# Conditioning totals over partitions: TensorE transposes and VectorE sums in place of products with a column of ones

## The reference, cut to what matters

```python
def adaln_mod(cond, w, b):
    m = jax.nn.silu(cond) @ w + b
    m = m.reshape(m.shape[0], 1, 6, D_MODEL)
    return tuple(m[:, :, j] for j in range(6))

sh1_p, sc1_p, g1_p, sh2_p, sc2_p, g2_p = adaln_mod(c_ctx[None, :], ada_w[i], ada_b[i])
sh1_s, sc1_s, g1_s, sh2_s, sc2_s, g2_s = adaln_mod(c, ada_w[i], ada_b[i])
```

## Time and profile before

| | |
|---|---|
| median of 3 runs | 2580.86 us (2577.29 to 2583.99) |
| the profiled execution, its own time | 2578.82 us |
| its span in the trace | 2577.0 us |
| PE busy | 2324.0 us, 90% of the span |
| DVE busy | 1793.2 us, 70% |
| ACT busy | 1304.5 us, 51% |
| mean granted TensorE clock | 0.954 of full speed |

### The profile page before, as it was taken

The page is one execution under the profiler, slowest core; times in us unless marked ns, Lnnn a source line. Parts: engine busy times, 40 slices in busy tenths (PEclk is TensorE's granted clock), DMA queues, the critical chain, the costliest instruction groups (busy, mean ns, idle before and its releaser), DMA issues.

```text
span 2577.0 us, 28840 instructions
## 1 busy us (share of the span) xinstructions
PE 2324.0 (90%) x9896; PEld 1537.3 (60%) x9896; DVE 1793.2 (70%) x2348; ACT 1304.5 (51%) x1698; POOL 336.5 (13%) x229
## 2 busy tenths in 40 slices
PE   6999999999957999999998688998859999999995
PEld 2867868678634666666665355554436666666663
DVE  3665655656657999999998512332368999999996
ACT  3222212222235877778776323332238778777773
POOL 1000000000021122112111200000221113231102
PEclk9999999999977999999999789999979999999997
DMA  7443435434236988998887210000138998888892
GB/s 250 131 123 108 148 96 164 131 115 141 90 129 221 354 319 312 348 344 330 322 314 264 87 68 0 34 1 1 63 119 316 349 350 332 333 327 315 331 343 88
DMA packets 167646, 529.04 MB, mean 205 GB/s; under 512 B 13525, under 2 KB 22282, under 8 KB 167306
## 3 DMA queue, kind: packets, MB, share of 16 engines
q1 hardware_dynamic: 162954, 515.35, 55.5%
q0 software_dynamic: 2304, 8.39, 0.9%
q10 hardware_dynamic: 2304, 4.20, 0.4%
HBM read 516.72 MB, written 11.17 MB: 205 GB/s over the span
## 4 chain that ended last, share of the span: by engine, by line
PE 70%; DVE 12%; issue 6%; DMA 5%; ACT 5%; POOL 1%; SPq 0%; ACTq 0%; DVEq 0%
PE ps L1511 67%; DVE W_LO L1321 6%; PE ps L1514 3%; DMA RAW_W<-in_moe_w_down_dram 3%; DMA RAW_W<-in_moe_w_gate_dram 2%; ACT YE_HI L290 1%; ACT GATE L853 1%; ACT W_HI L290 1%; DVE YE_LO L1339 1%; DVE B L1366 1%; POOL SMALL L560 1%; DVE IDX L1296 1%; DVE MIXREG L1295 0%; POOL SMALL L559 0%; DVE B L1099 0%
## 5 line engine op out<-in xcount | busy, mean ns | idle before, releaser
L1321 DVE TENSOR_TENSOR W_LO<-RAW_W,W_HI 128x1024 fp32r<-128x1024 f32 x768 | 901.4, 1220 | 81.6 <-ACT W_HI L290 75.1
L290 ACT ACTIVATE W_HI<-RAW_W 128x1024 fp32r<-128x1024 f32 x768 | 779.0, 1055 | 286.4 <-PE ps L1511 166.4
L1511 PE MATMUL ps<-W_HI,XET_HI 128*80 128x512 f32 x1024 | 331.9, 406 | 37.9 <-DVE W_LO L1321 18.6
L1511 PE MATMUL ps<-W_LO,XET_HI 128*80 128x512 f32 x1024 | 326.7, 401 | 0.0
L1511 PE MATMUL ps<-W_HI,XET_LO 128*80 128x512 f32 x1024 | 325.5, 400 | 0.0
L1511 PEld LDWEIGHTS ps<-W_HI,XET_HI 128*80 128x80 f32 x1024 | 153.2, 152 | 125.6 <-DVE W_LO L1321 26.8
L1511 PEld LDWEIGHTS ps<-W_LO,XET_HI 128*80 128x80 f32 x1024 | 155.9, 152 | 89.4 <-issue 7.7
L1511 PEld LDWEIGHTS ps<-W_HI,XET_LO 128*80 128x80 f32 x1024 | 154.8, 151 | 87.7 <-issue 6.0
L1070 DVE SCALAR_TENSOR_TENSOR ADA_SUM<-ADA_RAW,NCOL,ADA_SUM 128x512 f32<-128x512 f32 x280 | 191.3, 747 | 0.1
L1511 PE MATMUL ps<-W_HI,HTE_HI 128*80 128x512 f32 x512 | 164.7, 403 | 11.2 <-issue 11.2
L1511 PE MATMUL ps<-W_LO,HTE_HI 128*80 128x512 f32 x512 | 160.1, 394 | 0.0
(11 more groups left out here) (218 smaller groups left out, 3584.2 us busy)
## 6 DMA issues: line engine op xcount, KB each, us to landing
RAW_W<-in_moe_w_gate_dram SPq DMA_DIRECT2D x128, 1024.0 KB, 5.3
RAW_W<-in_moe_w_up_dram SPq DMA_DIRECT2D x128, 1024.0 KB, 6.1
RAW_W<-in_moe_w_down_dram SPq DMA_DIRECT2D x128, 1024.0 KB, 7.2
ADA_RAW<-in_ada_w_dram SPq DMA_DIRECT2D x80, 512.0 KB, 3.7
RING_RAW<-in_ret_w_in_dram SPq DMA_DIRECT2D x48, 512.0 KB, 4.2
W<-in_ada_w_dram SPq DMA_DIRECT2D x4, 2048.0 KB, 14.2
RING_RAW<-in_ret_w_out_dram SPq DMA_DIRECT2D x16, 512.0 KB, 4.6
xn_rows<-B SPq DMA_DIRECT2D x8, 512.0 KB, 12.8
```

The lines of the kernel that those rows point to most:

```text
L290: return nc.scalar.activation(out, in_, ACT.Copy, scale=scale)
L1321: V_.tensor_tensor(W_LO[:, slot], RAW_W[:, (place + i) // 2 % RAWS, at:at + PART], W_HI[:, slot].bitcast(F32), ALU.subtract).then_inc(MS_[ ...
L1511: return T.matmul(out, lhsT, rhs, start=first, stop=last)
```

## The change

The sum over partitions is done in another way. PE transposes each 128 by 128 block of `ADA_SUM`, so that the 512 columns of one conditioning vector fill one whole bank: partition = output column within the block, free axis = four blocks of 128 former partitions. DVE then sums along the free axis with two `tensor_reduce` instructions (one for each c, 512 values in and 4 out per partition), waits for them, and adds the bias in a third instruction that reads SBUF.

As each event now fills two banks instead of eight columns of one, `COLS_BANK` holds pairs, and some waits of PE change: the second event of a head waits until DVE has read the first (both use banks 4 and 5); the third waits for one more evacuated tile of scores; the y loop waits for the sums of the third event ahead of its first product, since that writes bank 6; the fourth event waits for the gate's evacuation (bank 2) instead of for the third's sums; the value tiles 2 and 3 both wait for the fifth event of the head before; gate tile 2 waits for the second event's sums instead of the first's.

```diff
-        COLS_BANK = (4, 5, 3, 3, 6)
+        COLS_BANK = ((4, 5), (4, 5), (3, 6), (3, 2), (6, 7))
...
-                parts = ps[:, COLS_BANK[t], 0:8].rearrange("p (q c) -> p q c", q=4)
-                V_.tensor_tensor(cols, parts, BCOL[:, layer, at].unsqueeze(2).to_broadcast([P, 4, 2]), ALU.add).then_inc(ada2_col, 1)
+                for c in range(2):
+                    last = V_.tensor_reduce(cols[:, :, c], ps[:, COLS_BANK[t][c], :].rearrange("p (q n) -> p q n", q=4), AX, ALU.add)
+                chain.link(last)
+                V_.tensor_tensor(cols, cols, BCOL[:, layer, at].unsqueeze(2).to_broadcast([P, 4, 2]), ALU.add).then_inc(ada2_col, 1)
...
-                for q in range(4):
-                    for c in range(2):
-                        at = 2 * q + c
-                        last = mm(ps[:, COLS_BANK[t], at:at + 1], ADA_SUMS[C % 2][:, c, q * P:(q + 1) * P], ONES[:, 0:1], True, True)
+                for c in range(2):
+                    for q in range(4):
+                        at = slice(q * P, (q + 1) * P)
+                        last = tr(ps[:, COLS_BANK[t][c], at], ADA_SUMS[C % 2][:, c, at])
                 last.then_inc(ada2_tr, 1)
...
                     if k in (2, 6):
-                        pe.wait_ge(qk_ev, 4 * h + 4)
+                        pe.wait_ge(*((qk_ev, 4 * h + 4) if k == 2 else (ada2_col, NT * h + 1)))
                         ada_columns2(h, k // 4)
...
-                        if k == 0 and t == 2 and h:
+                        if k == 0 and t in (2, 3) and h:
                             pe.wait_ge(ada2_col, NT * h)
...
                     if k == 6:
-                        pe.wait_ge(sc_ev, NT * h + 3)
+                        pe.wait_ge(sc_ev, NT * h + 4)
                         ada_columns2(h, 2)
...
-                            pe.wait_ge(*((v_ev, NT * h + 5), (sc_ev, NT * h + 1), (ada2_col, NT * h + 1), (ada2_col, NT * h + 2), (sc_ev, NT * h + 2))[t])
+                            pe.wait_ge(*((v_ev, NT * h + 5), (sc_ev, NT * h + 1), (ada2_col, NT * h + 2), (ada2_col, NT * h + 2), (sc_ev, NT * h + 2))[t])
...
                 pe.wait_ge(kp_ev, h + 1)
+                pe.wait_ge(ada2_col, NT * h + 3)
...
                     if t == 0:
-                        pe.wait_ge(ada2_col, NT * h + 3)
+                        pe.wait_ge(silg, NT * (h + 1))
                         ada_columns2(h, 3)
```

## The result

The changed kernel takes 2561.25 us (median of 6 runs, 2555.44 to 2566.6) beside 2579.07 us for the kernel before on the same chip (2575.88 to 2586.96): ratio 0.9925, 95% interval 0.9905 to 0.9945. Measured twice more, in 5 rounds each, it gave 2567.3 against 2581.44 us (0.9939, 0.9921 to 0.9956) and 2565.17 against 2579.84 us (0.9943, 0.9928 to 0.9958). The forecast was 2564.5 us.

What follows compares the result with a forecast made beforehand. PE was taken to bound the kernel, carrying 70% of the chain. Savings of 15.6 and 0.97 less 1.34 us gave -15.2: 2563.6 from the profiled 2578.82, or 2565.6 by the median; forecast 2564.5, range 2558 to 2572.

Steps and rivals of the forecast that it cites:

- PE sets the pace in the heads: In the heads, PE is busy 100.00 of 100 us, so the end moves with PE's work, microsecond for microsecond.
- Sixteen matmuls (eight products in two passes) for eight transposes, 0.82 us saved: On PE, each event falls from 1.70 to 0.88 us; 19 events in the heads give 15.6 us.
- The sums on DVE, +1.34 us per event: Two reductions, a wait and the bias addition take 1.51 us on DVE where 0.165 stood; 27 us in all.
- What hides them: DVE's idle stretches behind events in the heads cover the added work at no cost; tightest, 1.40 us left before second y's statistics.
- The moved waits: PE's changed waits in the heads are already reached when PE comes to them, so they cost nothing visible.
- Behind the heads, +0.37 us: The last event saves 0.97 us on PE, but its uncovered DVE sums between `ROWI` and `OHP` add 1.34.
- the half-clock stretch of 1.7 us: Just behind the last event the clock halves for 3.4 us, costing 1.7 us; it may move by as much either way.
- The sum: Whole kernel: -15.6 - 0.97 + 1.34 = -15.2 us, giving 2563.6 from the profiled execution; forecast put at 2564.5.
- Two-pass transposes: Transposes on PE run as 16 records at 0.107 us, so the heads gain nothing: 2580 us; chance 7%.
- the failing cover: DVE's sums delay PE at the scores and second y in four heads; 10.7 us come back: 2574 us; chance 5%.
- the falling clock in the heads: Transposed events halve the clock for 3.4 us, 1.7 us lost each; 19 falls give 2596 us; chance 6%.
- the second rival: DVE's cover fails at scores and second y, 2574 us; at twice the reduction rate only (2.78 - 2.74) us exposed; 5%.

Runs made afterwards that it cites:

- the event of 32: Changed kernel with each transpose done four times, 32 transposes per event: 2618.49 us, heads 684.32 us.

## Why the prediction was right, point by point

**PE sets the pace in the heads.** Right. Repeating the transposes adds their full price to the stretch, at 0.108 us each, while repeating the sums once adds nothing.

**Sixteen matmuls (eight products in two passes) for eight transposes, 0.82 us saved.** The mechanism was right, the term too small: 0.91 us by both views. I had 1.70 right for what goes; what comes takes 0.80 instead of 0.88. The pitch of 0.108 us was right, as the repeated transposes show, but the product behind follows the last transpose sooner than a whole pitch: the event of 32 takes 3.41 us, that is 32 x 0.109 less some 0.08. By that the heads should gain 19 x 0.91 = 17.3 us; they gained 17.3 to 17.9, where 15.6 were forecast. The bound that transposes don't overlap (2.18 us per event) did not come true, and with it falls the estimate from the Trainium skill's page "TensorE: Matmul & The Clock Gate", section "Part 4: PE-mode transpose": its 275 ns, given for bf16, agree with the recorded duration of one (272 ns here, fp32), but are not what one costs in a row.

**The sums on DVE, +1.34 us per event.** Right: a reduction lasts 686 ns on average against 692 worked out, the pair to the addition 1.33 us. The Trainium skill's page "VectorE: DVE Perf Modes", section "Rules for kernel authors", calls the reduction the slowest operation of DVE and says to consider restructuring; here 40 of them cost 1.3 us of time in all, since 38 are hidden.

**What hides them.** Right in the heads. The row on which most rested was the tightest one, 1.40 us forecast ahead of the second y's statistics and 1.32 measured; doubling the sums uses it up without a cost. That what exceeds the idle time goes to PE was too strict: with the sums five times DVE is some 3.6 us late there and PE waits 2.55. My reading of the margins did not carry as far as five times, where two places came late instead of one.

**The moved waits.** Right: no PE wait stands on them in the changed kernel, and with the products put back in the new banks and waits the heads take what they took before.

**Behind the heads, +0.37 us.** The event's -0.97 came out at -0.85 (1.85 to 1.00) and the sums' +1.34 at +1.33 (0.66 to 1.99 us of waiting). What I had left open either way, the half-clock stretch of 1.7 us, went: -1.7. That it went was not foretold. Together -1.2 us, of which the stretch as a whole shows -0.7 to -1.4.

**The sum.** By the measured terms it is -17.3 - 1.2 = -18.5 us instead of -15.2, or 2560.3 against the profiled execution of before. The forecast of 2564.5 had 0.9 added for the median of before; the three medians, 2561.25, 2567.3 and 2565.17, lie on both sides of it. The gains by the medians are 17.8, 14.1 and 14.7 us: all below the 18.5 of the measured terms, two of them by some 4 us. So that the forecast's 15.2 came out so close is in part luck. Its terms were too small by 1.7 us in the heads and by 1.6 behind them, and the whole time shows, on average over the three, some 3 us less than the two stretches gained. That the shift is carried to the end is thus shown as far as the first expert product; whether a part is given back behind it or the difference is scatter stays open.

**The rivals.** Two-pass transposes are out by the count of records and by the repeated transposes, the failing cover by the doubled sums, the falling clock in the heads by the 32 transposes in a row. The 2.78 us that the second rival sets against 2.74 can't be rebuilt exactly from its own terms (2 x 1.34 is 2.68, four reductions of 692 ns are 2.77); by either, next to nothing would be exposed, and with the doubled sums PE gets no new wait in the heads. The cover does have an end, though, and what then comes back is more than the sum of the waits, as the five-fold sums show.

## What to carry to other kernels

Where one engine is busy without a gap, count what each instruction holds it for from start to next start among its neighbours, not by its recorded duration: a transpose of 272 ns costs 108 here, and an fp32 product that writes a single column costs that twice, once for each of its two passes. The idle time ahead of the other engine's instructions gives a first measure of how much work may move to it: here 1.2 us more per event cost nothing, and at 4.9 us more the waits came back at two places per head and took the clock with them. And look for the one place where the same step has no cover: it may be worth moving it alone.

## What the runs showed of the hardware that I had not expected

Behind 1.64 us of idle time and sixteen one-column matmuls the granted clock falls to 1.2 GHz, in all three profiles that have them behind the heads (with the products put back everywhere it falls shortly before the event ends). Behind the same idle time and eight transposes in the same place it stays at 2.4 GHz, in all six profiles that have them. The length of the event does not decide it: sixteen transposes take 1.87 us, as long as the sixteen matmuls with their 1.85, and the clock stays up. But transposes don't always keep it up: 32 of them behind 1.94 us of idle time ran at 0.50 from 774.90 to 778.00, while 32 in the full stream of the heads ran at 1.00. What separates these two cases was not tested. The Trainium skill's page "TensorE: Matmul & The Clock Gate", section "Part 4: PE-mode transpose", says that transposes don't count as busy for the clock as products do. The 32 behind the heads would fit that; the heads don't show it, and in the last event it was the products behind which the clock fell.

A wait of 2.5 us in an otherwise full PE halved the clock afterwards in three of four heads with the same instructions and the same wait, and not in the fourth. So a short wait can cost some 1.7 us more than its length, and doesn't always.
